# GpSimd instead of VectorE makes the low halves of the next group's weights in a hybrid GLA/SSD layer

## The chip, the cores and the metric

One core of a Trainium2 chip runs the kernel. The metric is the device time of one execution in microseconds: 1674.93 us as the median of three runs before the change (1674.78 to 1676.38).

## The reference

One decoder layer over 2048 tokens of width 1024, in float32. A conditioning vector gives shift, scale and gate; the normalised input h goes through one projection `w_in`, whose columns belong to two kinds of heads: gated linear attention (GLA) and a Mamba-2 state-space part (SSD). Their outputs go through `w_out`, a norm, the gate and a residual sum. The change concerns the SSD part and how its weights, and those of the last projection, are made ready:

```python
xbc = jax.nn.silu(causal_depthwise_conv(xbc, conv_w[i], conv_b[i]))
xs, Bm, Cm = jnp.split(xbc, [SSD_INNER, SSD_INNER + SSD_GROUPS * SSD_STATE], axis=-1)
dt = jax.nn.softplus(dt_raw.astype(f32) + dt_bias[i].astype(f32))
...
y = ssd_chunked(xs_h, dt, A, Bm..., Cm...)       # per chunk of 128: decay-weighted C B^T x, plus C times state
y = y + d_skip[i].astype(f32)[:, None] * xs_h
y = y.reshape(Bsz, T, SSD_INNER).astype(x.dtype) * jax.nn.silu(z)
y = rms_norm(y.reshape(Bsz, T, SSD_GROUPS, SSD_INNER // SSD_GROUPS), ...)
mixed = jnp.concatenate([o, y], axis=-1) @ w_out[i]
```

## The kernel before, in words

**Three stages.** `front` does the norms, the GLA projections and the GLA heads, `ssd` (the recurrence) the SSD heads, `project_out` the product with `w_out` and the end. In the trace the recurrence lies from about 755 to 1372 us.

**Split matrices.** Each matrix product is made of three float32r products of halves: a number is split into a high part (a copy rounded by ScalarE) and a low part (the number minus its high part), and high*high, high*low and low*high are summed. `w_high` (L1580, ScalarE) makes the high part of a unit of weights, `w_low` (L1707, VectorE) the low part. `h_high` and `h_low` do the same for quarters of the activations h.

**Blocks and units.** The recurrence goes over two groups of SSD heads (g = 0, 1), and in each over 8 blocks of 256 tokens, so 16 blocks n = 0 to 15, and a tail step 16. In block n TensorE makes 8 units for the current tokens: units 0 to 5 (B, C and four of x; 128 columns of weights each, 24 matmuls of 256 columns), and two z units (u = 6, 7; 24 matmuls of 512 columns). Between these units it does the recurrence of block n - 1, for its two tiles of 128 tokens, t = 0 and 1: `tile_in(0)` ahead of unit 0, `tile_out(0)` and `tile_in(1)` ahead of unit 2, `tile_out(1)` ahead of unit 4, `turn(0)` (the transposes of the normalised row block c_yn, L1930) ahead of unit 6, `turn(1)` at the end. Each engine's program is written out in this order by the same loop over u, and each executes its own in order; semaphores tie them.

**ScalarE in a block** (L1654): after unit u it evacuates the bank (`evacuate`: copies to c_before and c_acc, L1607 and L1609); TensorE's unit u + 2 waits for that, since there are two banks. Then, only in the last block of a group, `w_high` of the next group's unit u (in block 15, where the next stage's weights are made, `w_high(G, u - 1)`). Then, in some slots, `h_high`, `square` (u = 3 and 5) and `normed` (u = 4 and 6), which makes c_yn out of the c_rstd of GpSimd.

**VectorE in a block** (L1807): `tile_in` (c_xdt, c_xd, c_decay, c_btok), three taps of convolution for each unit (`convolve`, L1741), `tile_out` (c_yi, c_state, c_yt, twice), `segments` (16 instructions, L1802), `h_low`, and, in the last block of a group, `w_low` right behind the convolution of each unit.

**GpSimd in a block's recurrence** (L1556): for each tile `ends` (c_xend), `decay_state` (c_decayed, once c_state is ready), `skip` (c_yi + c_xd, once VectorE has made c_yi); then `rstd_of` for both tiles (c_mse, c_rstd, once ScalarE's square is there), then c_y_diff. GpSimd's step r belongs to the recurrence of block r, which the other engines do beside the units of block r + 1.

**Loads.** SyncE issues all loads in one order (L1477). w_raw has two slots; `load_w(g, u)` goes to slot u % 2 and waits until the low part of unit u - 2 has been made (`wait(sp, w_ready, order(g, u) - 1)`, L1436). In block 7 it issues loads 0, 1, 2, then a quarter of h, load 3, a quarter, loads 4 and 5, a quarter, load 6, a quarter, load 7. Units of w_in are 128x1024 (512 KB), those of the projection's w_sums 128x512 (256 KB). Units 6 and 7 of group 1 are z parts; their low parts are made in block 8.

Of the kernel before, what the change touches and what calls it, by code (L numbers as in the profile page):

```python
# [17 lines left out]
F32 = mybir.dt.float32  # L18
# [3 lines left out]
ALU = mybir.AluOpType  # L22
# [3 lines left out]
HI, LO = 0, 1  # L26
# [5 lines left out]
def wait(eng, sem, count):  # L32

    if not isinstance(count, int) or count > 0:
        eng.wait_ge(sem, count)
# [1306 lines left out]
def ssd(nc, sems, handed, y_stored, unit_done, h_ready, xd_ready, w_rows, w_sum_d, conv_col, convb_col, d_row, norm_col, ps, ident, tok, w, w_raw, hl_all, halves, w_even,  # L1342
        h_d, ac_d, y_d, column, T, KT, G, HG, GW, XT, NS, SP_, INNER, VAL, TAPS, B2, TB2):

    UB, UC, UX, UZ = 0, 1, 2, 2 + XT
# [3 lines left out]
    S = T // B2  # L1349
# [7 lines left out]
    NF = KT  # L1357
    with ExitStack() as ctx:
# [3 lines left out]
        def sem(name):  # L1362
            return sems.enter_context(nc.semaphore(name))
# [35 lines left out]
        w_hi = sem("c_w_hi"); w_ready = sem("c_w_ready"); unit_out = sem("c_unit_out")  # L1399
# [14 lines left out]
        def part(u, p):  # L1414

            return w[:, u, :, p, :] if u < UZ else w_z[:, :, p, (u - UZ) * P:(u - UZ + 1) * P]
# [5 lines left out]
        def order(g, u):  # L1422

            return u - UZ if g == 0 else g * U - UZ + u
# [87 lines left out]
        def gpsimd(pool):  # L1512
            pool.wait_ge(handed["att_done"], handed["last_scores"])
            pool.wait_ge(handed["again_low"], handed["h_parts"])
            pool.memset(past[:, :], 0.0).then_inc(consts_ready, 1)
            pool.memset(before[:, :, 0:HIST], 0.0).then_inc(consts_ready, 1)
            pool.wait_ge(consts_ready, 2)
            pool.affine_select(out=past[:, :], in_=past[:, :], compare_op=ALU.is_ge, fill=-1e30,
                               base=0, pattern=[[1, P]], channel_multiplier=-1).then_inc(consts_ready, 1)
            pool.wait_ge(handed["y_stored"], handed["all_y"])  # L1520
            pool.memset(neg_half[:, :], -0.5).then_inc(consts_ready, 1)
            pool.wait_ge(consts_ready, 4)

            def ends(r, g, b, t):

                m = r * TB2 + t
                pool.wait_ge(xdt_ready, m + 1)
                wait(pool, st_done, m)
                end = tok[:, bass.ds(b * TB2 + t, 1), 3, g * HG:(g + 1) * HG].rearrange("p a h -> p (a h)")
                pool.tensor_tensor(xend[:, :, :], xdt[:, :, :], end.unsqueeze(2).broadcast_to([P, HG, SP_]),  # L1530
                                   ALU.mult).then_inc(xend_ready, 1)

            def decay_state(r, g, t):
                m = r * TB2 + t
                pool.wait_ge(decay_ready, r + 1)
                pool.wait_ge(state_ready, m + g + 1)
                pool.tensor_tensor(decayed[:, :, :], state[:, :, :], chunk[:, :, t:t + 1].broadcast_to([P, HG, SP_]),
                                   ALU.mult).then_inc(decayed_ready, 1)

            def skip(r, t):  # L1540

                m = r * TB2 + t
                pool.wait_ge(xd_ready, m + 1)
                pool.wait_ge(yi_ready, m + 1)
                pool.tensor_tensor(yi[:, :, :], yi[:, :, :], xd[:, :, :], ALU.add).then_inc(skip_ready, 1)  # L1545

            def rstd_of(r, t):
                m = r * TB2 + t
                pool.wait_ge(ms_ready, m + 1)
                pool.sem_inc(passed, 1)  # L1550
                pool.tensor_scalar(mse[:, t:t + 1], ms[:, t:t + 1], EPS, None, ALU.add).then_inc(mse_ready, 1)
                pool.wait_ge(mse_ready, m + 1)
                wait(pool, yn_ready, m)
                pool.tensor_tensor(rstd[:, t:t + 1], mse[:, t:t + 1], neg_half[:, :], ALU.pow).then_inc(rstd_ready, 1)  # L1554

            def step(r, g, b):  # L1556

                for t in range(TB2):
                    ends(r, g, b, t)
                    decay_state(r, g, t)  # L1560
                    skip(r, t)
                for t in range(TB2):
                    rstd_of(r, t)
                pool.wait_ge(y_ready, r * TB2 + TB2)
                wait(pool, y_stored, r * 32)
                pool.tensor_tensor(y_diff[:, :, :], y[:, 0], y[:, 1], ALU.subtract).then_inc(diff_ready, 1)

            for g in range(G):
                step(g * S, g, 0)
                with pool.Fori(1, S) as i:  # L1570
                    step(i + g * S, g, i)

        def scalar(act):

# [131 lines left out]
        def vector(dve):  # L1706
            def w_low(g, u):  # L1707
                dve.wait_ge(w_hi, order(g, u) + 1)
                if g < G:
                    dve.tensor_tensor(part(u, LO), w_raw[:, u % 2], part(u, HI).bitcast(F32),  # L1710
                                      ALU.subtract).then_inc(w_ready, 1)
                else:
                    dve.tensor_tensor(w_even[:, u, LO, :], w_raw[:, u % 2, 0:KT // 2].rearrange("p k n -> p (k n)"),
                                      w_even[:, u, HI, :].bitcast(F32), ALU.subtract).then_inc(w_ready, 1)
# [41 lines left out]
            def tile_in(r, g, b, t):  # L1756
                m = r * TB2 + t
                dve.wait_ge(x_done, m + 1)
                wait(dve, y_done, m)
                wait(dve, xend_ready, m)  # L1760
                dve.tensor_tensor(xdt[:, :, :], bank(X), per_head(b, t, 0, g), ALU.mult).then_inc(xdt_ready, 1)  # L1761
                wait(dve, skip_ready, m)
                skips = d_row[:, g * HG:(g + 1) * HG].unsqueeze(2).broadcast_to([P, HG, SP_])
                dve.tensor_tensor(xd[:, :, :], bank(X), skips, ALU.mult).then_inc(xd_ready, 1)
                dve.wait_ge(bc_done, m + 1)
                dve.wait_ge(decay_ready, r + 1)
                dve.tensor_tensor(decay[:, :, t * P:(t + 1) * P], ps[:, BC, NS:NS + P].unsqueeze(1).broadcast_to([P, HG, P]),  # L1767
                                  decay[:, :, t * P:(t + 1) * P], ALU.mult)
                wait(dve, st_done, m)
                dve.tensor_copy(btok[:, :], ps[:, BC, 0:NS]).then_inc(wt_ready, 1)  # L1770

            def clear_state(r):
                wait(dve, yi_done, r * TB2)
                wait(dve, decayed_ready, r * TB2)
                dve.memset(state[:, :, :], 0.0).then_inc(state_ready, 1)
# [31 lines left out]
            def step(n, g, b, par, rg, rb, first_of_group, last_of_group):  # L1807


                going, back = g is not None, rg is not None  # L1810
                if back and first_of_group:
                    clear_state(n - 1)
                if isinstance(n, int) and n == 1:
                    dve.wait_ge(handed["y_stored"], handed["all_y"])
                for u in range(UP):
                    if back and u == 0:
                        tile_in(n - 1, rg, rb, 0)
                    if back and u == 2:
                        tile_out(n - 1, rg, rb, 0, 1 - par)
                        tile_in(n - 1, rg, rb, 1)  # L1820
                    if back and u == 4:
                        tile_out(n - 1, rg, rb, 1, 1 - par)
                    if g == 0 and rg is None and u in Z_SLOTS[0]:
                        w_low(0, UZ + Z_SLOTS[0].index(u))
                    if going and u < UZ:
                        convolve(n, g, u)
                        if u == UZ - 1:
                            history(n, last_of_group)
                    if going and u == UZ:
                        segments(n, g, b)  # L1830
                    if g == 1 and rg == 0 and u in Z_SLOTS[1]:
                        w_low(1, UZ + Z_SLOTS[1].index(u))
                    if last_of_group and g + 1 < G and u < UZ:
                        w_low(g + 1, u)
                    if last_of_group and g + 1 == G and u > 0:
                        w_low(G, u - 1)
                    if not going and u == 0:
                        w_low(G, NF - 1)
                    if back and u in H_SLOTS:
                        h_low(n + 1, H_SLOTS.index(u), 1 - par)  # L1840
# [13 lines left out]
        def tensor(pe, part):  # L1854
# [107 lines left out]
            step(G * S, None, 0, G - 1, 0)  # L1962

        return sync, gpsimd, scalar, vector, tensor


# [319 lines left out]
```

## Time and profile before

| | |
|---|---|
| median of three runs (lowest to highest) | 1674.93 us (1674.78 to 1676.38) |
| span of the profiled execution | 1675.5 us; the page gives no other time for it |
| TensorE busy | 1612.1 us, 96% of the span |
| VectorE busy | 1052.7 us, 63% |
| ScalarE busy | 841.1 us, 50% |
| GpSimd busy | 396.7 us, 24% |
| DMA, mean | 138 GB/s |

The shares are averages over three stages. A profile of this kind is to be read stage by stage: the stretches of single blocks, then what TensorE waited for in them, then each engine's instructions in order of time. In the rows a start in us stands first, then the time that the merged instructions took, the engine, the line, the operation, output and inputs, the count, and in brackets the idle time just before and what ended it.

### The profile page before, as it was taken

How to read it: one execution, taken by the hardware profiler on the slowest of the kernel's cores; microseconds unless marked ns; L12 is line 12 of the kernel's file. 1: busy time of each engine (PE TensorE's matmuls, PEld its weight loads, DVE VectorE, ACT ScalarE, POOL GpSimd, SP SyncE). 2: the span in 40 equal slices, each digit the busy share in tenths (PEclk: the TensorE clock that was granted, in tenths of full speed). 3: DMA queues.
4: the chain of work that ended last, by engine and by line, in shares of the span. 5: the costliest groups of instructions: out<-in, count | busy, mean ns of one | idle time of the engine just before them, and what ended most of it. 6: DMA issues, size and time to landing. Idle time of an engine off the chain costs nothing. (4 is left out here: it accounts for less than half of the span.)

```text
span 1675.5 us, 27425 instructions
## 1 busy us (share of the span) xinstructions
PE 1612.1 (96%) x9990; PEld 1387.5 (83%) x9990; DVE 1052.7 (63%) x1754; ACT 841.1 (50%) x1496; POOL 396.7 (24%) x449
## 2 busy tenths in 40 slices
PE   5999999999999999998999998999999999999997
PEld 4888888888888888888888887888888878888886
DVE  5545354465444554456777777867777754785996
ACT  5755555545544554464454555555454554234332
POOL 2311000101322222200223222223233220450423
PEclk9899999999999999999999999999999999999999
DMA  9423442264434533334222225322212326765886
GB/s 327 134 93 108 143 125 65 79 189 145 157 126 135 189 121 129 124 104 145 76 71 76 75 75 152 112 85 99 76 69 75 108 97 210 241 237 169 291 288 199
DMA packets 131358, 231.14 MB, mean 138 GB/s; under 512 B 9907, under 2 KB 81859, under 8 KB 126134
## 3 DMA queue, kind: packets, MB, share of 16 engines
q1 hardware_dynamic: 123910, 190.76, 35.2%
q10 hardware_dynamic: 6512, 38.80, 6.2%
q0 software_dynamic: 832, 0.22, 0.3%
q8 instruction: 62, 1.02, 0.2%
q14 instruction: 42, 0.34, 0.1%
HBM read 177.05 MB, written 52.70 MB: 137 GB/s over the span
## 5 line engine op out<-in xcount | busy, mean ns | idle before, releaser
L1155 PE MATMUL ps<-hl,w 128*128 128x512 f32 x1488 | 374.5, 401 | 0.1
L1155 PEld LDWEIGHTS ps<-hl,w 128*128 128x128 f32 x1488 | 275.1, 189 | 56.8 <-issue 1.4
L1870 PE MATMUL ps<-hl,w 128*128 128x256 f32 x2304 | 293.0, 287 | 0.0
L1870 PEld LDWEIGHTS ps<-hl,w 128*128 128x128 f32 x2304 | 280.6, 192 | 7.9 <-issue 7.8
L1161 PE MATMUL ps<-w,hl 128*128 128x256 f32 x1536 | 200.6, 287 | 0.0
L1161 PEld LDWEIGHTS ps<-w,hl 128*128 128x128 f32 x1536 | 190.6, 191 | 2.3
L1874 PE MATMUL ps<-hl 128*128 128x512 f32 x768 | 180.9, 395 | 4.5 <-DVE hl L1710 4.5
L1741 DVE SCALAR_TENSOR_TENSOR c_acc<-c_before,conv_col,c_acc 128x256 f32<-128x256 f32 x288 | 161.5, 563 | 36.9 <-ACT c_acc L1609 30.0
L1874 PEld LDWEIGHTS ps<-hl 128*128 128x128 f32 x768 | 144.7, 190 | 34.5 <-DVE hl L1710 4.7
L2259 PE MATMUL ps<-w,hl 128*128 128x512 f32 x720 | 164.1, 389 | 0.0
L2259 PEld LDWEIGHTS ps<-w,hl 128*128 128x128 f32 x720 | 135.0, 188 | 28.2 <-issue 0.3
L485 POOL TENSOR_SCALAR mse<-ms 128x1 f32<-128x1 f32 x60 | 15.6, 260 | 543.2 <-ACT squares L655 543.2
L1607 ACT ACTIVATE c_before<-ps 128x256 f32<-128x256 f32 x96 | 36.9, 384 | 209.2 <-PE ps L1870 209.2
L2259 PE MATMUL ps<-hl 128*128 128x512 f32 x576 | 131.0, 389 | 0.0
L2259 PEld LDWEIGHTS ps<-hl 128*128 128x128 f32 x576 | 108.1, 188 | 22.5
L902 DVE SCALAR_TENSOR_TENSOR state<-state,dec,ps 128x256 f32<-128x256 f32 x56 | 26.9, 480 | 108.1 <-PE ps L1198 108.1
L841 DVE TENSOR_TENSOR hl<-x_sb,hl 128x1024 fp32r<-128x1024 f32 x48 | 59.3, 1235 | 56.5 <-ACT hl L639 56.5
L2215 DVE TENSOR_TENSOR d_mixed<-d_mixed,ps 128x512 f32<-128x512 f32 x64 | 42.5, 683 | 53.3 <-PE ps L2259 34.5
L1545 POOL TENSOR_TENSOR c_yi<-c_yi,c_xd 128x512 f32<-128x512 f32 x32 | 41.4, 1293 | 131.7 <-DVE c_yi L1781 131.7
L914 DVE SCALAR_TENSOR_TENSOR y<-ps,norm_col,gz 128x128 f32<-128x128 f32 x120 | 36.3, 344 | 56.1 <-PE ps L1206 35.7
L852 DVE TENSOR_TENSOR w<-w_raw,w 128x1024 fp32r<-128x1024 f32 x30 | 37.5, 1252 | 50.2 <-ACT w L585 50.1
L1802 DVE SCALAR_TENSOR_TENSOR c_decay<-c_ac,tok,c_past 128x128 f32<-128x128 f32 x256 | 68.6, 347 | 0.1
(247 smaller groups left out, 2613.8 us busy)
## 6 DMA issues: line engine op xcount, KB each, us to landing
x_sb<-h SPq DMA_DIRECT2D x52, 512.0 KB, 3.9
w_raw<-in_w_in SPq DMA_DIRECT2D x44, 512.0 KB, 4.7
c_ac<-step_sums ACTq DMA_DIRECT2D x16, 1024.0 KB, 4.6
d_a_raw<-mixed_in SPq DMA_DIRECT2D x29, 512.0 KB, 4.1
c_h_raw<-h SPq DMA_DIRECT2D x56, 256.0 KB, 2.9
d_a_raw<-mixed_in SPq DMA_DIRECT2D x11, 1024.0 KB, 5.0
w_sums<-late ACTq DMA_DIRECT2D x8, 1280.0 KB
w_raw<-w_sums SPq DMA_DIRECT2D x40, 256.0 KB, 3.4
```

Source lines behind the costliest of these rows:

```text
L841: last = dve.tensor_tensor(hl[:, n % 2, ks, LO, :], raw, hl[:, n % 2, ks, HI, :].bitcast(F32), ALU.subtract)
L852: dve.tensor_tensor(lo, w_raw[:, u % 2], hi.bitcast(F32), ALU.subtract).then_inc(w_ready, 1)
L1155: mm = pe.matmul(ps[:, PROJ + u % 2, :], w[:, u, k, a, :], hl[:, par, k, b, :], start=(k == 0 and i == 0), stop=(k == KT - 1 and i == 2))
L1161: mm = pe.matmul(ps[:, PROJ + u % 2, half * DV:(half + 1) * DV], hl[:, par, k, a, t * P:(t + 1) * P], w_v[:, k, b, :], start=(k == 0 and i ...
L1545: pool.tensor_tensor(yi[:, :, :], yi[:, :, :], xd[:, :, :], ALU.add).then_inc(skip_ready, 1)
L1607: act.activation(before[:, u, HIST:], ps[:, PROJ + u % 2, 0:B2], ACT.Copy)
L1741: op = dve.scalar_tensor_tensor(out=acc[:, u, :], in0=before[:, u, k:k + B2], scalar=conv_col[:, k, ch:ch + 1], in1=acc[:, u, :], op0=ALU. ...
L1802: last = dve.scalar_tensor_tensor(out=decay[:, h, t * P:(t + 1) * P], in0=ac[:, h, t * P:(t + 1) * P], scalar=own, in1=past[:, :], op0=ALU ...
L1870: mm = pe.matmul(ps[:, PROJ + u % 2, 0:B2], w[:, u, k, a, :], hl[:, par, k, b, :], start=(k == 0 and i == 0), stop=(k == KT - 1 and i == 2))
L1874: mm = pe.matmul(ps[:, PROJ + u % 2, :], hl[:, par, k, a, t * P:(t + 1) * P], w_z[:, k, b, :], start=(k == 0 and i == 0), stop=(k == KT - ...
L2215: last = dve.tensor_tensor(mixed[:, p, r, c, :], old, bank, ALU.add if how > 0 else ALU.subtract)
L2259: mm = pe.matmul(ps[:, j % 8, :], halves[:, j % 4, k, a, :], weight(i)[:, k, b, :], start=(k == 0 and q == 0), stop=(k == KT - 1 and q == 2))
```

## The change

In the steps of the recurrence that run beside the last block of a group (block 7, where group 0 gives way to group 1, and block 15, where group 1 gives way to the projection), GpSimd makes the low parts that VectorE made: units 0 to 5 of group 1's weights, and units 0 to 6 of the projection's. VectorE keeps the z parts of group 1 (made in block 8) and unit 7 of the projection (made in the tail), and waits ahead of the first of either until the counter w_ready has all the earlier ones. GpSimd's loop over blocks becomes shorter by two steps for each group, and these two are written out.

```diff
+            def w_low(g, u):
+                pool.wait_ge(w_hi, order(g, u) + 1)
...
+                pool.tensor_tensor(lo, raw, hi.bitcast(F32), ALU.subtract).then_inc(w_ready, 1)
+
-            def step(r, g, b):
+            def step(r, g, b, before_last):
 
                 for t in range(TB2):
                     ends(r, g, b, t)
                     decay_state(r, g, t)
+                    if before_last and t == 1:
+                        w_low(g + 1, 0)
                     skip(r, t)
                 for t in range(TB2):
+                    for u in ((1,), (2, 3))[t] if before_last else ():
+                        w_low(g + 1, u)
                     rstd_of(r, t)
+                for u in range(4, 6 if g + 1 < G else 7) if before_last else ():
+                    w_low(g + 1, u)
                 pool.wait_ge(y_ready, r * TB2 + TB2)
...
             for g in range(G):
-                step(g * S, g, 0)
-                with pool.Fori(1, S) as i:
-                    step(i + g * S, g, i)
+                step(g * S, g, 0, False)
+                with pool.Fori(1, S - 2) as i:
+                    step(i + g * S, g, i, False)
+                step(g * S + S - 2, g, S - 2, True)
+                step(g * S + S - 1, g, S - 1, False)
...
             def w_low(g, u):
                 dve.wait_ge(w_hi, order(g, u) + 1)
+                if g > 0 and u in (UZ, NF - 1):
+                    dve.wait_ge(w_ready, order(g, u))
...
-                    if last_of_group and g + 1 < G and u < UZ:
-                        w_low(g + 1, u)
-                    if last_of_group and g + 1 == G and u > 0:
-                        w_low(G, u - 1)
                     if not going and u == 0:
                         w_low(G, NF - 1)
```

The order of GpSimd's instructions in its step beside block 7, with the changed kernel's own line numbers (L1563 is the new low part; c_xend, c_decayed, c_yi are `ends`, `decay_state`, `skip`, here of tile 1):

```order
L1530 TENSOR_TENSOR c_xend<-c_xdt,tok 128x512
L1537 TENSOR_TENSOR c_decayed<-c_state,c_chunk 128x512
L1563 TENSOR_TENSOR w<-w_raw,w 128x8x128
L1545 TENSOR_TENSOR c_yi<-c_yi,c_xd 128x512
L1563 TENSOR_TENSOR w<-w_raw,w 128x8x128
L1551 TENSOR_SCALAR c_mse<-c_ms 128x1
L1554 TENSOR_TENSOR c_rstd<-c_mse,c_neg_half 128x1
L1563 TENSOR_TENSOR w<-w_raw,w 128x8x128 x2
```

Four of the six low parts are here: unit 0 ahead of the second tile's `skip`, unit 1 behind it, units 2 and 3 behind the first tile's c_rstd; 4 and 5 follow behind the second tile's.

VectorE's order in block 7, kernel before, from the first convolution (c_acc) to the first tile's c_yi:

```order
L1741 SCALAR_TENSOR_TENSOR c_acc<-c_before,conv_col,c_acc 128x256 x3
L1710 TENSOR_TENSOR w<-w_raw,w 128x8x128
L1741 SCALAR_TENSOR_TENSOR c_acc<-c_before,conv_col,c_acc 128x256 x3
L1710 TENSOR_TENSOR w<-w_raw,w 128x8x128
L1725 TENSOR_TENSOR hl<-c_h_raw,hl 128x2x256
L1781 TENSOR_TENSOR c_yi<-ps,tok 128x512
```

and the same place in the changed kernel, from the end of `tile_in(0)` to the first tile's c_yt:

```order
L1789 COPY c_btok<-ps 128x128
L1760 SCALAR_TENSOR_TENSOR c_acc<-c_before,conv_col,c_acc 128x256 x6
L1744 TENSOR_TENSOR hl<-c_h_raw,hl 128x2x256
L1800 TENSOR_TENSOR c_yi<-ps,tok 128x512
L1803 TENSOR_TENSOR c_state<-ps,c_decayed 128x512
L1807 TENSOR_TENSOR c_yt<-ps,c_yi 128x512
```

The two low parts that stood between the convolutions of units 0 and 1 and the first tile's c_yi are gone from VectorE. TensorE, ScalarE and SyncE keep their order.

## Rows read from the trace of the kernel before

**Rows 1.** Stretches (us, busy by engine, clock, DMA): loop step, block 7.

```profile
976.00:1012.24 36.24, 36.24 (x286) 31.63 (x285) 27.15 (x55) 18.74 (x37) 10.36 (x12) 1.00 0.23 79
...
1012.24:1052.45 40.21, 35.45 (x260) 29.81 (x260) 31.28 (x57) 21.84 (x38) 9.71 (x11) 0.96 0.52 151
```

**Rows 2.** TensorE in order of time, block 7: start, us, work, idle before it.

```profile
1029.74 1.88 PE L1917 MATMUL ps<-c_xdt,c_decay 128*64 128x64 f32 x32 [3.73 <-DVE c_btok L1770]
...
1040.16 0.66 PE L1930 MATMUL ps<-ident,c_yn 128*128 128x128 f32 x4 [0.88 <-ACT c_yn L1640]
...
1040.57 11.17 PE L1874 MATMUL ps<-hl 128*128 128x512 f32 x48
```

**Rows 3.** ScalarE in order of time, block 7.

```profile
1019.37 0.56 ACT L1609 ACTIVATE c_acc<-ps,convb_col,conv_col 128x256 f32<-128x256 f32 x1
...
1024.15 1.06 ACT L1585 ACTIVATE w<-w_raw 128x1024 fp32r<-128x1024 f32 x1 [1.41 <-DMA w_raw<-in_w_in]
...
1025.90 0.56 ACT L1609 ACTIVATE c_acc<-ps,convb_col,conv_col 128x256 f32<-128x256 f32 x1
...
1037.91 1.06 ACT L1585 ACTIVATE w<-w_raw 128x1024 fp32r<-128x1024 f32 x1 [0.63 <-DMA w_raw<-in_w_in]
...
1042.19 0.62 ACT L1633 ACTIVATE c_squares<-c_yt 128x512 bf16<-128x512 f32 x1
```

**Rows 4.** VectorE in order of time, block 7.

```profile
1013.26 3.03 DVE L1741 SCALAR_TENSOR_TENSOR c_acc<-c_before,conv_col,c_acc 128x256 f32<-128x256 f32 x3 [1.47 <-ACT c_acc L1609]
...
1019.23 1.23 DVE L1710 TENSOR_TENSOR w<-w_raw,w 128x1024 fp32r<-128x1024 f32 x1 [2.94 <-ACT w L1585]
...
1021.80 1.22 DVE L1710 TENSOR_TENSOR w<-w_raw,w 128x1024 fp32r<-128x1024 f32 x1
...
1027.08 0.69 DVE L1761 TENSOR_TENSOR c_xdt<-ps,tok 128x512 f32<-128x512 f32 x1
...
1032.98 1.52 DVE L1741 SCALAR_TENSOR_TENSOR c_acc<-c_before,conv_col,c_acc 128x256 f32<-128x256 f32 x3
...
1035.55 0.69 DVE L1781 TENSOR_TENSOR c_yi<-ps,tok 128x512 f32<-128x512 f32 x1
```

**Rows 5.** GpSimd in order of time, block 7.

```profile
1014.26 1.23 POOL L1537 TENSOR_TENSOR c_decayed<-c_state,c_chunk 128x512 f32<-128x512 f32 x1
...
1028.95 1.05 POOL L1537 TENSOR_TENSOR c_decayed<-c_state,c_chunk 128x512 f32<-128x512 f32 x1
...
1043.44 0.79 POOL L1554 TENSOR_TENSOR c_rstd<-c_mse,c_neg_half 128x1 f32<-128x1 f32 x1
```

**Rows 6.** GpSimd by line: ns min/median/max, first and last start.

```profile
L1566 POOL TENSOR_TENSOR c_y_diff<-c_y x16: 1284/1294/1302, 829.0 to 1373.4; 128x512 f32<-128x512 f32 x16
...
L2118 POOL TENSOR_TENSOR d_a_raw<-d_a_raw x16: 2391/2738/3133, 1428.2 to 1597.5; 128x1024 f32<-128x1024 f32 x16
```

**Rows 7.** Loads of w_raw, L1438 (512 KB), then L1440 (256 KB): issue to landing.

```profile
DMA to landing us min/median/max: 3.6/4.4/8.1
...
DMA to landing us min/median/max: 2.6/2.7/3.2
```

**Rows 8.** Order of time, block 15: VectorE, GpSimd, ScalarE, TensorE.

```profile
1332.51 0.69 DVE L1781 TENSOR_TENSOR c_yi<-ps,tok 128x512 f32<-128x512 f32 x1
...
1333.34 1.30 POOL L1545 TENSOR_TENSOR c_yi<-c_yi,c_xd 128x512 f32<-128x512 f32 x1 [5.31 <-DVE c_yi L1781]
...
1334.07 0.63 ACT L1588 ACTIVATE w<-w_raw 128x512 fp32r<-128x512 f32 x1
...
1336.41 0.66 PE L1930 MATMUL ps<-ident,c_yn 128*128 128x128 f32 x4 [0.23 <-ACT c_yn L1640]
```

**Rows 9.** TensorE's first z units, then a stretch behind the 3.73 us wait.

```profile
775.72 13.54 PE L1874 MATMUL ps<-hl 128*128 128x512 f32 x48 [4.52 <-DVE hl L1710]
...
1031.60:1033.00 1.40, 1.40 (x5) 0.79 (x3) 1.40 (x3) 0.00 (x0) 0.00 (x0) 0.50 0.00 0
```

**Rows 10.** TensorE in order of time, the tail behind block 15.

```profile
1362.73 1.15 PE L1917 MATMUL ps<-c_xdt,c_decay 128*64 128x64 f32 x32 [1.72 <-DVE c_btok L1770]
```

More of the change, by code:

```diff
@@ L1554, in rstd_of @@
                 pool.tensor_tensor(rstd[:, t:t + 1], mse[:, t:t + 1], neg_half[:, :], ALU.pow).then_inc(rstd_ready, 1)
-            def step(r, g, b):
+            def w_low(g, u):
+                pool.wait_ge(w_hi, order(g, u) + 1)
+                if g < G:
+                    hi, lo, raw = w[:, u, :, HI, :], w[:, u, :, LO, :], w_raw[:, u % 2]
+                else:
+                    hi, lo = w_even[:, u, HI, :], w_even[:, u, LO, :]
+                    raw = w_raw[:, u % 2, 0:KT // 2].rearrange("p k n -> p (k n)")
+                pool.tensor_tensor(lo, raw, hi.bitcast(F32), ALU.subtract).then_inc(w_ready, 1)
+            def step(r, g, b, before_last):
                 for t in range(TB2):
```

## The prediction, made before the changed kernel ran

> **What bounds the kernel now.** I read the stretches first, then the waits of TensorE, then the four compute engines in order of time around the two places where the change acts. Most steps of the recurrence are bound by TensorE: it is busy 36.24 of 36.24 us in a step of the loop [rows 1], and VectorE, ScalarE and GpSimd wait for it. The step in which group 0 gives way to group 1 (block 7; its `w_low` calls make the low halves of group 1's units 0 to 5) is different: TensorE is busy 35.45 of 40.21 us [rows 1]. Two gaps are named: 3.73 us before the y products, until VectorE has written c_btok, and 0.88 us before the transposes of c_yn [rows 2]. In the step before the projection (block 15) only 0.23 us are lost at the same transposes [rows 8]. So there is little to win, at most the two gaps.
>
> What the reader must see next is a ring that goes through those same engines. w_raw has two slots. The load of unit u+2 waits for the low part of unit u; ScalarE's `w_high(u+2)` waits for that load; and ScalarE works strictly in the order of its program, in which `w_high` stands between things TensorE needs: the evacuation of the next unit, `square`, `normed`. Before, low(0) ends at 1020.46 on VectorE and w_high(2) starts at 1024.15, having waited 1.41 us for the transfer; w_high(4) waited 0.63 us for its own [rows 3, 4]. The ring has no slack here already. Whatever delays low(0), (1), (2) by more than that delays ScalarE, and ScalarE's c_yn is what the TensorE queue stands behind at 1040.16 [rows 2].
>
> **What is removed.** VectorE loses 6 lows of 1.2 us in block 7 and 7 lows of 0.69 us in block 15. In block 7 only the first two lie ahead of c_btok: c_acc of unit 1 is done at 1019.37 + 0.56 = 1019.93 [rows 3], so convolve(1) starts some 0.4 us sooner, and low(1) gives 1.2. The 3.73 us wait becomes 2.1. That saving stays only if nothing later in the step is late; it isn't so.
>
> **What is added, block 7.** I follow the new order. On GpSimd low(0) stands behind xend(1) and decayed(1) of tile 1, not at unit 0. A GpSimd low of 128x1024 is not in the trace. A GpSimd subtraction or sum of the same size took 2.39 us at least and 2.74 as median; twice the 128x512 one is 2 x 1.294 = 2.6 [rows 6]. Bounds 2.4 and 3.1 (longest of the rows of that size); I take 2.6. From low's end to the start of `w_high` of the next unit in the slot I take 3.7 us (1020.46 to 1024.15 [rows 3, 4]); landing alone took 3.6 to 8.1, median 4.4 [rows 7], so 3.7 is near the low end, right for a load that has no other one beside it.
> 1. c_xdt(1) was at 1027.08 [rows 4], now 1.6 us earlier, 1025.5. decayed(1) ended at 1028.95 + 1.05 = 1030.0 [rows 5], now 1028.4. low(0) ends at 1031.0; I add 0.3 for its turns with VectorE: 1031.3, against 1020.46.
> 2. Load 2, 3.7 us: w_high(2) starts at 1035.0 (was 1024.15). h_high and c_acc(3) follow, 1025.90 + 0.56 - 1024.15 = 2.3 us after it [rows 3]: 1037.3. VectorE waits for it with h_low and convolve(3), 1.5 us [rows 4]: yi(1) at 1038.8 (was 1035.55).
> 3. `skip(1)` on GpSimd starts 0.83 us after yi and takes 1.3 (1332.51, 1333.34 [rows 8] show the pair): 1040.9. Only then low(1): 1043.5 (was 1023.0).
> 4. Load 3, 3.7 us: w_high(3) at 1047.2, one us of work, square(0) at 1048.2. `rstd_of` ends 2.0 us after the start of its square (1042.19 to 1043.44 + 0.79 [rows 3, 5]): 1050.2. low(2), queued behind it: 1052.8.
> 5. Load 4, 3.7 us: w_high(4) at 1056.5 (was 1037.91). From there to TensorE's c_yn transposes 2.25 us (1037.91 to 1040.16 [rows 2, 3]): 1058.8 against 1040.16, **18.6 us later**.
> Meanwhile TensorE does the y products, unit 4, waits for c_acc(3), does unit 5 until about 1040.3 and stands still for 18 us. Its order is fixed: the two z units behind the transposes can't go first. What comes after shifts with it: low(4) and (5) end near 1069, ahead of block 8, and loads 6 and 7 near 1067 and 1069, about 5 us later than the shift alone would make them; ScalarE needs their data at about 1056.59 + 18.6 + the clock's share, so they still land. VectorE's 16 segments lie beside lows 4 and 5; c_decay has some 2 us of room. Nothing more is charged.
>
> **The clock.** Behind today's 3.73 us wait a stretch shows a granted clock of 0.50, that is 1.2 instead of 2.4 GHz, and behind a 4.52 us wait at the first block the two z units took 13.54 us instead of 11.17 [rows 2, 9]. After 18 us idle the same fall before the same z units is due: 13.54 - 11.17 = 2.4 us more. The slow stretch inside today's step lies ahead of the new end of the chain, so its going or staying changes nothing. Block 7 in all: 18.6 + 2.4 = 21.0.
>
> **Block 15.** `w_high` stands one unit later, loads and lows are half the size. VectorE reaches yi(1) 1.5 us sooner (lows 0 to 2 are off it; 1332.51 to 1331.0), skip ends at 1333.1, low(1) of 1.3 us at 1334.4. A load of this size lands in 2.6 to 3.2 us [rows 7]; with its issue 3.0: w_high(3) at 1337.4 (was 1334.07). From there to the transposes it is the 2.25 us of block 7 less 0.43 for the half-sized w_high (1.06 and 0.63 [rows 3, 8]), 1.8: 1339.3 against 1336.41 [rows 8], +2.9. low(2) follows rstd(0) and its load lands near 1339.9, just when ScalarE is there. The 3.2 us gap may drop the clock: 0 to 2.4, I take 1.2. In the tail low(6) no longer stands ahead of c_xdt on VectorE, and of TensorE's 1.72 us wait there [rows 10] I give back 1.2. Block 15 in all: +2.9.
>
> **Sum.** 21.0 + 2.9 = 23.9. The profiled execution spans 1675.5 us, 0.6 above the median of 1674.93, so 1675.5 + 23.9 = 1699.4 in its terms, 1698.8 in those of the median: **1699**. Bounds: with lows of 2.4, no 0.3, no clock, block 15 at +1.0: 18.6 - 0.9 + 1.0 = 18.7. With three lows of 3.1 and three loads at 4.4: 18.6 + 1.5 + 2.1 + 2.4, and block 15 at +5.5: 30. This is 1693 to 1705.
>
> **The skill weighed against the row.** convolve(0), begun at 1013.26, took 3.03 us for three taps while GpSimd made c_decayed, against 1.52 alone [rows 4, 5]: VectorE is held up while GpSimd runs. The Trainium skill, SBUF — State Buffer, section "Who interferes with whom", says that a VectorE instruction with two SBUF inputs and a GpSimd one that reads SBUF exclude each other for a whole instruction, and the one that came first wins. The trace agrees in kind. By that rule each GpSimd low would also block VectorE for its 2.6 us, so moving 1.2 us of VectorE work costs VectorE more than it frees wherever it has work; here it mostly waits then. The sum by it alone would be at most 1 us higher for each of the lows 0 and 1, 1701.
>
> **Rivals.**
> - *The ring bites deeper* (14%). Lows at 3 us and over, loads over 4.4 us since they now meet the state and c_h_raw transfers, and block 15 loses its clock too: 28 to 34 us, 1703 to 1709; about 1706. For: landings up to 8.1 us [rows 7]. Against: there is one load in flight at a time now.
> - *It bites half* (11%). Only one round of the ring is felt, because low(1) goes before skip(1)'s input is late, or w_high(3) overlaps TensorE's wait: 8 to 14 us, about 1686. For: TensorE itself could be at the transposes at 1040 only. Against: each of the three rounds has its own GpSimd predecessor (decayed(1), skip(1), rstd(0)), and each of these waits for ScalarE or VectorE.
> - *Faster, the relief decides* (3%). VectorE's 3.73 us gap shrinks by 1.6, the slow clock behind it goes (1.6 us), the tail gives 1.2: 4.4 us, 1670.5. It decides if low(2) is done by 1034.2, that is w_high(4) no later than 1037.91. Against: low(0) alone can't start before 1028.
> - *Nothing is felt* (2%): the chain is hidden under z units, 1675. Against: the transposes stand ahead of the z units.
> - The forecast (70%): 1691 to 1706.
>
> **Chances.** 0.2% of the time is 3.3 us, about what can be told from no change. Faster 3%, same 2%, slower 95%. The range 1688 to 1707 leaves out the faster and the unchanged case, most of the half case and the tail of the deep one.
>
> **What would show it.** TensorE's wait for ACT c_yn near 18 us at the first place and 3 at the second; ScalarE's waits for `w_raw` of about 12 us before w_high(2), 10 before w_high(3), 6 before w_high(4); GpSimd rows of 2.6 and 1.3 us; 13.5 us for the z units of block 7. It is wrong if w_high(3) there starts less than 6 us after c_acc(3), or if low(0) starts before c_decayed(1).

## The result: 26 us slower

| | before | changed |
|---|---|---|
| median of four (lowest to highest) | 1674.86 us (1673.97 to 1676.38) | 1700.9 us (1700.78 to 1701.83) |
| span of the profiled execution | 1675.5 us | 1699.3 us |
| ratio of the runs | | 1.0152 (95% interval 1.014 to 1.0164) |

The forecast was 1699 with 1688 to 1707. The first rows of the page of the changed kernel: span, busy time of each engine, granted clock in 40 slices.

```profile
span 1699.3 us, 27402 instructions
...
PE 1615.4 (95%) x9990; PEld 1390.4 (82%) x9990; DVE 1053.7 (62%) x1741; ACT 841.1 (49%) x1496; POOL 421.8 (25%) x462
...
PEclk9999999999999999999999997999999999999999
```

TensorE's busy time is nearly what it was, GpSimd has 25 us more and VectorE as much as before, though 13 low halves (some 12 us) have left it: what it does beside GpSimd takes longer. The clock row has one slice at 7.

**Where the time is, by blocks.** Since the two profiled executions differ by 1.4 us before the change acts, I compare lengths. A block begins with TensorE's first transposes of c_xbc; for block 15 and the tail I take the last c_yn transposes of the block before.

| | before | changed | difference |
|---|---|---|---|
| block 7 | 43.48 (1008.54 to 1052.02) | 64.42 (1007.12 to 1071.54) | +20.9 |
| block 8 | 39.78 | 39.53 | -0.3 |
| blocks 9 to 14 | 219.44 | 219.44 | 0 |
| block 15 | 37.01 | 42.42 | +5.4 |
| tail, to the first product of the projection | 24.01 | 23.10 | -0.9 |

The sum is +25.2, between the difference of the spans (23.8) and that of the medians (26.0). Less the 1.4 us ahead of block 7 it is the difference of the spans. A span and a median of times can't be subtracted from each other, as the prediction did with its "0.6 above the median": in the later runs of the kernel before, an execution's time is 1.7 to 1.8 us more than its span, so by that estimate the profiled one took about 1677.2 us, over 2 us more than the median. The forecast itself starts from the median. The table also corrects a row of mine: the second stretch of [rows 1], called block 7, starts 3.7 us inside it and ends 0.4 us behind it. The block really took 43.5 us, 6.9 more than a step of the loop, so there was a little more to win than the prediction said. No term of its sum came from that row.

TensorE in block 7 of the changed kernel, in the columns of [rows 2]:

```profile
1026.78 1.15 PE L1932 MATMUL ps<-c_xdt,c_decay 128*64 128x64 f32 x32 [2.59 <-DVE c_btok L1789]
...
1028.42 3.43 PE L1885 MATMUL ps<-hl,w 128*128 128x256 f32 x24
...
1035.99 5.49 PE L1885 MATMUL ps<-hl,w 128*128 128x256 f32 x24 [4.14 <-ACT c_acc L1626]
...
1057.21 1.11 PE L1945 MATMUL ps<-ident,c_yn 128*128 128x128 f32 x4 [15.73 <-ACT c_yn L1657]
...
1057.97 13.29 PE L1889 MATMUL ps<-hl 128*128 128x512 f32 x48
...
1071.10 0.60 PE L1945 MATMUL ps<-ident,c_yn 128*128 128x128 f32 x4
```

The 3.73 us wait for c_btok of [rows 2] is now 2.59, then comes a wait that wasn't there, 4.14 us ahead of unit 5 for ScalarE's c_acc(3), and the wait ahead of the c_yn transposes is 15.73 us instead of 0.88. Unit 5 itself ran slowly (5.49 us against 3.1). The z units took 13.29 us instead of 11.17.

ScalarE, GpSimd and VectorE in the same block:

```profile
1033.63 1.06 ACT L1602 ACTIVATE w<-w_raw 128x1024 fp32r<-128x1024 f32 x1 [12.31 <-DMA w_raw<-in_w_in]
...
1035.38 0.56 ACT L1626 ACTIVATE c_acc<-ps,convb_col,conv_col 128x256 f32<-128x256 f32 x1
...
1046.01 1.06 ACT L1602 ACTIVATE w<-w_raw 128x1024 fp32r<-128x1024 f32 x1 [10.08 <-DMA w_raw<-in_w_in]
...
1046.97 0.61 ACT L1650 ACTIVATE c_squares<-c_yt 128x512 bf16<-128x512 f32 x1
...
1054.97 1.06 ACT L1602 ACTIVATE w<-w_raw 128x1024 fp32r<-128x1024 f32 x1 [6.57 <-DMA w_raw<-in_w_in]
...
1056.45 0.71 ACT L1657 ACTIVATE c_yn<-c_yt,c_rstd 128x512 f32<-128x512 f32 x1
```

```profile
1025.88 1.05 POOL L1537 TENSOR_TENSOR c_decayed<-c_state,c_chunk 128x512 f32<-128x512 f32 x1
...
1026.88 2.55 POOL L1563 TENSOR_TENSOR w<-w_raw,w 128x1024 fp32r<-128x1024 f32 x1
...
1038.24 1.28 POOL L1545 TENSOR_TENSOR c_yi<-c_yi,c_xd 128x512 f32<-128x512 f32 x1 [8.81 <-DVE c_yi L1800]
...
1039.47 2.37 POOL L1563 TENSOR_TENSOR w<-w_raw,w 128x1024 fp32r<-128x1024 f32 x1
...
1048.18 0.57 POOL L1554 TENSOR_TENSOR c_rstd<-c_mse,c_neg_half 128x1 f32<-128x1 f32 x1
...
1048.71 4.88 POOL L1563 TENSOR_TENSOR w<-w_raw,w 128x1024 fp32r<-128x1024 f32 x2
```

```profile
1011.84 3.03 DVE L1760 SCALAR_TENSOR_TENSOR c_acc<-c_before,conv_col,c_acc 128x256 f32<-128x256 f32 x3 [1.47 <-ACT c_acc L1626]
...
1024.11 0.68 DVE L1780 TENSOR_TENSOR c_xdt<-ps,tok 128x512 f32<-128x512 f32 x1
...
1026.64 3.59 DVE L1760 SCALAR_TENSOR_TENSOR c_acc<-c_before,conv_col,c_acc 128x256 f32<-128x256 f32 x3
...
1037.41 0.68 DVE L1800 TENSOR_TENSOR c_yi<-ps,tok 128x512 f32<-128x512 f32 x1
...
1060.09 8.60 DVE L1821 SCALAR_TENSOR_TENSOR c_decay<-c_ac,tok,c_past 128x128 f32<-128x128 f32 x16
```

This is the ring, step by step. L1563 is GpSimd's low half; "low(0)" is short for the low half of unit 0, c_yi(1) for c_yi of tile 1. low(0) begins at 1026.88 behind c_decayed(1); w_high(2) (L1602) has then waited 12.31 us for its transfer, and VectorE's c_yi(1) comes at 1037.41. `skip(1)` lets low(1) begin at 1039.47; w_high(3) has waited 10.08. Its square gives c_rstd at 1048.18, low(2) begins at 1048.71; w_high(4) has waited 6.57. c_yn follows at 1056.45, and TensorE goes on at 1057.21. In [rows 3] the waits before w_high(2) and (4) were 1.41 and 0.63 us.

The clock of the first part of the z units (columns as in [rows 1]; the clock is the figure third from the end):

```profile
1057.30:1061.00 3.70, 3.70 (x11) 3.12 (x12) 2.95 (x9) 3.70 (x7) 0.77 (x2) 0.50 0.25 71
```

It is 0.50, the lower of the two levels (1.2 instead of 2.4 GHz), behind the long wait.

Block 15 of the changed kernel, in the engines' order of [rows 8], then the tail:

```profile
1346.47 2.50 DVE L1760 SCALAR_TENSOR_TENSOR c_acc<-c_before,conv_col,c_acc 128x256 f32<-128x256 f32 x3
...
1350.93 0.68 DVE L1800 TENSOR_TENSOR c_yi<-ps,tok 128x512 f32<-128x512 f32 x1
...
1351.76 1.29 POOL L1545 TENSOR_TENSOR c_yi<-c_yi,c_xd 128x512 f32<-128x512 f32 x1 [3.58 <-DVE c_yi L1800]
...
1353.01 1.30 POOL L1563 TENSOR_TENSOR w<-w_raw,w 128x512 fp32r<-128x512 f32 x1
...
1357.65 0.63 ACT L1605 ACTIVATE w<-w_raw 128x512 fp32r<-128x512 f32 x1 [4.19 <-DMA w_raw<-w_sums]
...
1359.46 1.11 PE L1945 MATMUL ps<-ident,c_yn 128*128 128x128 f32 x4 [4.01 <-ACT c_yn L1657]
...
1360.23 12.42 PE L1889 MATMUL ps<-hl 128*128 128x512 f32 x48
...
1386.63 1.15 PE L1932 MATMUL ps<-c_xdt,c_decay 128*64 128x64 f32 x32 [0.90 <-DVE c_btok L1789]
```

The transposes waited 4.01 us, the z units behind them took 12.42 us (11.15 in the profile before), and the tail's wait for c_btok fell from the 1.72 us of [rows 10] to 0.90.

### The profile page after: what moved, and what is told of

Same layout as the page of the kernel before. It is cut to its first block and busy times, and to the rows that moved or that the text cites. A ratio compares the mean times of both kernels' runs of the same rounds, so it can differ in the third digit from the quotient of the medians.

```text
span 1699.3 us, 27402 instructions
## 1 busy us (share of the span) xinstructions
PE 1615.4 (95%) x9990; PEld 1390.4 (82%) x9990; DVE 1053.7 (62%) x1741; ACT 841.1 (49%) x1496; POOL 421.8 (25%) x462
## 3 DMA queue, kind: packets, MB, share of 16 engines
q1 hardware_dynamic: 123910, 190.76, 34.9%
## 5 line engine op out<-in xcount | busy, mean ns | idle before, releaser
L1760 DVE SCALAR_TENSOR_TENSOR c_acc<-c_before,conv_col,c_acc 128x256 f32<-128x256 f32 x288 | 168.6, 587 | 47.4 <-ACT c_acc L1626 40.4
L1821 DVE SCALAR_TENSOR_TENSOR c_decay<-c_ac,tok,c_past 128x128 f32<-128x128 f32 x256 | 74.0, 365 | 0.1
L1780 DVE TENSOR_TENSOR c_xdt<-ps,tok 128x512 f32<-128x512 f32 x32 | 22.0, 687 | 77.6 <-PE ps L1913 77.6
```

The costliest lines, as they stand in the source:

```text
L1760: op = dve.scalar_tensor_tensor(out=acc[:, u, :], in0=before[:, u, k:k + B2], scalar=conv_col[:, k, ch:ch + 1], in1=acc[:, u, :], op0=ALU. ...
L1821: last = dve.scalar_tensor_tensor(out=decay[:, h, t * P:(t + 1) * P], in0=ac[:, h, t * P:(t + 1) * P], scalar=own, in1=past[:, :], op0=ALU ...
```

## The experiments

The theory to be tested (A): the place of the low halves in GpSimd's program makes the ring of load, high half and low half late, and ScalarE, which stands in it in front of the evacuations and of c_yn, hands that to TensorE. The rivals: (B) a low half on GpSimd lasts twice as long and holds VectorE up, and that costs wherever it stands; (C) the weights themselves come late.

### One place at a time

Only block 7 (against the changed kernel), and the mirror of it for block 15:

```diff
-                step(g * S + S - 2, g, S - 2, True)
+                step(g * S + S - 2, g, S - 2, g == 0)
...
+                    if last_of_group and g + 1 == G and u > 0:
+                        w_low(G, u - 1)
```

> Only block 7's low halves are on GpSimd, block 15's are back on VectorE. By the traces block 7 costs 20.9 us and block 15 4.5: 1674.9 + 20.9 = 1695.8 (1694.5 to 1697.5). If the two places interact (what block 7 delays is caught up or paid again later) it lies outside.

Measured: 1695.49 us (1693.86 to 1695.68), the kernel before beside it 1674.49; ratio 1.0125 (1.0108 to 1.0142). +21.0, as expected.

> Only block 15's low halves are on GpSimd, block 7's are back on VectorE: 1674.9 + 4.5 = 1679.4 (1678 to 1681). If block 15's effect is only the clock behind a wait that block 7 prepared, it is under 1 us.

Measured: 1679.64 us (1678.2 to 1681.28), ratio 1.0028 (1.0017 to 1.0039). +5.2, and its block 15 is 41.59 us long, 4.6 over before, with a tail 0.9 shorter, so that its trace places 3.7 of the 5.2. In the changed kernel block 15 was 0.8 longer still: from the end of low(1) to w_high(3) it took 3.3 us there and 2.6 here (1335.14 to 1337.76). The two runs add up to 26.2, the cost of both changes together, so within the spread of the runs the places don't interact.

### The same late places, but no low half on GpSimd

Against the kernel before:

```diff
                         tile_out(n - 1, rg, rb, 1, 1 - par)
+                        if last_of_group and g + 1 < G:
+                            w_low(g + 1, 1)
...
-                    if last_of_group and g + 1 < G and u < UZ:
-                        w_low(g + 1, u)
+                    if last_of_group and g + 1 < G:
+                        if u == 2:
+                            dve.wait_ge(decayed_ready, (n - 1) * TB2 + 2)
+                            w_low(g + 1, 0)
+                        if u == 4:
+                            dve.wait_ge(rstd_ready, (n - 1) * TB2 + 1)
+                            w_low(g + 1, 2)
+                            w_low(g + 1, 3)
+                        if u == 5:
+                            dve.wait_ge(rstd_ready, (n - 1) * TB2 + 2)
+                            w_low(g + 1, 4)
+                            w_low(g + 1, 5)
```

> VectorE makes block 7's low halves, but at the points at which GpSimd made them in the changed kernel: low(0) once c_decayed(1) is there, (1) behind tile_out(1), (2) and (3) once the first c_rstd is there, (4) and (5) once the second is; block 15 as before the change. Theory A: the ring is as late though no low half is on GpSimd: low(0) and (1) end at the same time as there, (2) 1.3 us sooner: +17 and 2 for the clock, 1674.9 + 19 = 1694 (1690 to 1697). Theory B: GpSimd's duration and the holding up of VectorE are gone, so at most 1680.

Measured: 1696.41 us (1694.43 to 1697.24), ratio 1.0132 (1.0115 to 1.0149): +21.9, as much as with GpSimd in block 7. VectorE's low halves (L1710), ScalarE's w_high(2), (3), (4) (L1585) and TensorE's transposes:

```profile
1025.90 1.22 DVE L1710 TENSOR_TENSOR w<-w_raw,w 128x1024 fp32r<-128x1024 f32 x1
...
1038.58 1.22 DVE L1710 TENSOR_TENSOR w<-w_raw,w 128x1024 fp32r<-128x1024 f32 x1
...
1047.79 2.35 DVE L1710 TENSOR_TENSOR w<-w_raw,w 128x1024 fp32r<-128x1024 f32 x2
...
1031.27 1.06 ACT L1585 ACTIVATE w<-w_raw 128x1024 fp32r<-128x1024 f32 x1 [12.22 <-DMA w_raw<-in_w_in]
...
1043.92 1.06 ACT L1585 ACTIVATE w<-w_raw 128x1024 fp32r<-128x1024 f32 x1 [10.35 <-DMA w_raw<-in_w_in]
...
1052.92 1.06 ACT L1585 ACTIVATE w<-w_raw 128x1024 fp32r<-128x1024 f32 x1 [6.60 <-DMA w_raw<-in_w_in]
...
1055.16 1.12 PE L1942 MATMUL ps<-ident,c_yn 128*128 128x128 f32 x4 [18.39 <-ACT c_yn L1640]
```

The three waits are 12.22, 10.35 and 6.60 us, those of the changed kernel within 0.3. Its block 7 (from 1004.85) is 64.47 us long, against 64.42. Counted from the beginning of the block, the low halves compare like this:

| | start of low(0), (1), (2) | end of low(0), (1), (2) |
|---|---|---|
| GpSimd, changed kernel | 19.8, 32.4, 41.6 | 22.3, 34.7, 44.0 |
| VectorE, this run | 21.1, 33.7, 42.9 | 22.3, 34.9, 44.1 |

VectorE needs half the time, but in this order it gets to each low half 1.3 to 1.4 us later, and the ends are the same within 0.2. (The expectation had low(2) end 1.3 us sooner, but it stands behind a convolution; that is a part of why 21.9 was measured and not 19.) So a late end costs the same whichever engine makes the low half, and with no low half on GpSimd there is nothing to hold VectorE up: that part of B isn't needed for block 7. GpSimd's longer operation isn't ruled out as a part of the lateness. In the changed kernel the three low halves took 7.4 us on GpSimd, and on VectorE from the same starts they would have taken 3.7; by this estimate up to 3.7 of the 18.5 us of delay are duration and the rest is place. No run separates the two. The shorter loops of GpSimd's program aren't a cause either: this run doesn't have them and is as slow, and the last run below has them without this cost.

### GpSimd, but as early as the high halves allow

Against the changed kernel:

```diff
+            LOWS = (((0, 1), (2,), (3,), (), (4,), (5,)), ((0,), (1,), (2,), (), (3,), (4, 5, 6)))
...
-                    if before_last and t == 1:
-                        w_low(g + 1, 0)
+                    lows(t)
+                    if t == 1:
+                        lows(2)
                     skip(r, t)
                 for t in range(TB2):
-                    for u in ((1,), (2, 3))[t] if before_last else ():
-                        w_low(g + 1, u)
+                    lows(3 + t)
                     rstd_of(r, t)
...
+                lows(5)
```

> GpSimd makes the same low halves as in the changed kernel, but each as soon as ScalarE has made the high half: in block 7 low(0) and low(1) ahead of skip(0), low(2) ahead of skip(1), low(3) right behind it, (4) behind the first c_rstd, (5) last; in block 15 low(0) ahead of skip(0), (1) and (2) ahead of skip(1), (3) behind the first c_rstd. Theory A (the place in GpSimd's order closes the ring through the two w_raw slots): nearly all of the 26 us goes; VectorE is held up by low(0) and (1), so 2 to 6 us over the kernel before, 1677 to 1681, and ScalarE's wait before w_high(2) falls from 12.3 to about 2 us. Theory B (a low half of 2.5 us instead of 1.2, and VectorE held up while GpSimd runs, are what costs, wherever they stand): 1693 or more.

Measured: 1682.44 us (1681.47 to 1684.41), ratio 1.005 (1.0033 to 1.0067). 18 of the 26 us are gone; +8 stays, more than the 2 to 6 I expected. TensorE in block 7:

```profile
1024.74 1.13 PE L1930 MATMUL ps<-c_state,c_xbc 128*128 128x512 f32 x2 [2.05 <-DVE c_state L1808]
...
1029.58 1.98 PE L1937 MATMUL ps<-c_xdt,c_decay 128*64 128x64 f32 x32 [3.72 <-DVE c_btok L1794]
...
1042.66 0.66 PE L1950 MATMUL ps<-ident,c_yn 128*128 128x128 f32 x4 [2.97 <-ACT c_yn L1662]
...
1043.08 11.15 PE L1894 MATMUL ps<-hl 128*128 128x512 f32 x48
```

VectorE's convolutions of units 1 and 2:

```profile
1017.81 5.07 DVE L1765 SCALAR_TENSOR_TENSOR c_acc<-c_before,conv_col,c_acc 128x256 f32<-128x256 f32 x3 [3.58 <-ACT c_acc L1631]
...
1029.45 5.56 DVE L1765 SCALAR_TENSOR_TENSOR c_acc<-c_before,conv_col,c_acc 128x256 f32<-128x256 f32 x3
```

The wait of 15.73 us is 2.97, and ScalarE's before w_high(2) fell to 2.67, but a 2.05 us wait for c_state is new, the 3.72 us for c_btok stands as before, and c_yn is late by 2.97 instead of 0.88. Block 7 is 48.02 us long (+4.5), block 15 37.98 (+1.0), the tail 24.62 (+0.6); these and block 8 make 6.5 of the 8, the rest isn't placed. The 4.5 of block 7 are VectorE held up, the second half of B. Three taps take 5.07 us beside low(0) and (1), and VectorE reaches `h_low` 1.9 us later in the block than before, which is what c_state and c_btok are late by. The next three take 5.56 us beside low(2) and (3), both of which are ahead of skip(1), and cost 2.7 us more: SyncE issues load 4 behind a quarter of h that waits for `h_low`, so w_high(4) and c_yn come late. So B is real too where TensorE waits for VectorE; in the changed kernel's block 7 VectorE was waiting itself.

### ScalarE's high halves later

Against the run with only block 7 on GpSimd:

```diff
-                        if last and g + 1 < G and u < UZ:
+                        if last and g + 1 < G and u < 2:
                             w_high(g + 1, u)
...
                         normed(n - 1, 0)
+                    if last and g + 1 < G and u == 4:
+                        w_high(g + 1, 2)
+                    if last and g + 1 < G and u == 5:
+                        w_high(g + 1, 3)
                     if back and u == 5:
                         square(n - 1, 1)
...
+                    if last and g + 1 < G and u == 6:
+                        w_high(g + 1, 4)
...
+                    if last and g + 1 < G and u == 7:
+                        w_high(g + 1, 5)
```

> As the run with only block 7's low halves on GpSimd, in the changed kernel's GpSimd order, but ScalarE makes block 7's high halves 2 to 5 later: (2) behind normed(0), (3) ahead of square(1), (4) behind the evacuation of unit 6, (5) behind that of unit 7. The ring load, high, low is as long as before; ScalarE no longer stands in it ahead of the evacuations and of c_yn. Theory A (the ring reaches TensorE through ScalarE's order): the 21 us go nearly all, 1674.5 + 1 to 2 = 1676 (1673 to 1679). Theory C (the weights themselves come late, wherever ScalarE waits): the lateness shows at block 8's units, 1690 or more.

Measured: 1679.75 us (1677.38 to 1680.73), the kernel before beside it 1675.68; ratio 1.0023 (1.0013 to 1.0033). Of the 21 us 17 are gone, with GpSimd's program untouched. TensorE's transposes of block 7, its units and c_btok wait of block 8, then ScalarE's c_yn and w_high(2):

```profile
1038.68 0.66 PE L1955 MATMUL ps<-ident,c_yn 128*128 128x128 f32 x4 [2.50 <-ACT c_yn L1657]
...
1055.84 3.10 PE L1895 MATMUL ps<-hl,w 128*128 128x256 f32 x24 [1.50 <-ACT c_z L1631]
...
1073.29 1.15 PE L1942 MATMUL ps<-c_xdt,c_decay 128*64 128x64 f32 x32 [3.01 <-DVE c_btok L1797]
...
1037.91 0.72 ACT L1657 ACTIVATE c_yn<-c_yt,c_rstd 128x512 f32<-128x512 f32 x1 [3.20 <-POOL c_rstd L1554]
...
1038.54 1.04 ACT L1602 ACTIVATE w<-w_raw 128x1024 fp32r<-128x1024 f32 x1
```

c_yn now comes first and w_high(2) behind it, with no wait left for its transfer. Block 7 is 43.83 us long, 0.35 over before. But block 8 is 44.20, 4.4 over: TensorE waits 1.50 us for ScalarE's c_z and 3.01 for c_btok there, since high half (4) pushes ScalarE's c_decay and with it c_z back, and high half (5), low(5) and c_y_diff lie in it. What is put off is paid for later, in part. This isn't C: TensorE waits there for c_z, c_xend, c_btok and c_yn, and the trace puts none of its waits down to a weight. In all it is 4.1 over the kernel before instead of 1 to 2: the mechanism was right, what it is paid with in block 8 was left out.

### Loads sooner, and both together

Against the kernel before, all low halves on VectorE:

```diff
                 if group_ends:
-                    for u in (0, 1, 2):
-                        load_w(g + 1, u)
+                    load_w(g + 1, 2)
...
+                if isinstance(s, int) and s == S - 2:
+                    for u in (0, 1):
+                        load_w(g + 1, u)
                 if not (isinstance(s, int) and s == 0):
                     store_y(n - 1, g, s - 1)
```

> The kernel before (all low halves on VectorE), with loads 0 and 1 of the next weights issued one step earlier, behind the last quarter of h of the step before, so that w_high(0) in block 7 doesn't wait 4.9 us for its transfer. Theory: convolve(1) and with it c_btok come 2.6 us sooner, and the slow clock behind the 3.7 us wait goes (1.6 us): 1674.5 - 4 = 1670.5 (1669 to 1672). If low(0) and (1) on VectorE alone make the wait, it stays near 1674.

Measured: 1671.67 us (median of 11 runs; the kernel before beside it 1675.68), ratio 0.9982 (0.9973 to 0.9991): **faster than the kernel before**, by 3 us by the ratio and 4 by the medians. w_high(0), w_high(4) and TensorE's two waits in block 7:

```profile
1010.42 1.06 ACT L1587 ACTIVATE w<-w_raw 128x1024 fp32r<-128x1024 f32 x1
...
1032.26 1.06 ACT L1587 ACTIVATE w<-w_raw 128x1024 fp32r<-128x1024 f32 x1 [2.27 <-DMA w_raw<-in_w_in]
...
1024.04 1.15 PE L1919 MATMUL ps<-c_xdt,c_decay 128*64 128x64 f32 x32 [1.13 <-DVE c_btok L1772]
...
1034.50 0.66 PE L1932 MATMUL ps<-ident,c_yn 128*128 128x128 f32 x4 [2.51 <-ACT c_yn L1642]
```

w_high(0) has no wait. c_btok is waited for 1.13 us instead of 3.73, and the slow clock behind it is gone. c_yn is waited for 2.51 us instead of 0.88, so that block 7 is 40.51 us long: 3.0 less than before, not 4. What the step gained at one wait came partly back at the next, since w_high(4) waits 2.27 us for its transfer: SyncE issues load 4 behind a quarter of h that waits for VectorE's `h_low`.

Together with later high halves and GpSimd's low halves (low(1) and (2) behind the first c_rstd, (3) to (5) behind the second):

```diff
-                    for u in ((1,), (2, 3))[t] if before_last else ():
-                        w_low(g + 1, u)
+                    if t == 1 and before_last:
+                        w_low(g + 1, 1)
+                        w_low(g + 1, 2)
                     rstd_of(r, t)
-                for u in range(4, 6 if g + 1 < G else 7) if before_last else ():
+                for u in (3, 4, 5) if before_last else ():
```

> Early loads and the later high halves together, block 7's low halves on GpSimd: (0) behind c_decayed(1), (1) and (2) behind the first c_rstd, (3) to (5) behind the second; high half (3) behind silu_conv; block 15's low halves on VectorE. VectorE has no low half ahead of c_btok(1): of the 6.9 us by which block 7 is longer than a step of the loop (43.5 against 36.6) some 5 go: 1669.5 (1667.5 to 1672). If GpSimd's low halves hold VectorE up ahead of c_yi(1) as much as they free it, it is no faster than the run with early loads alone.

Measured: 1675.04 us (1673.33 to 1676.76), ratio 0.9997 (0.9988 to 1.0006), no change from before and 3.4 us slower than early loads alone. TensorE in block 8:

```profile
1050.96 4.51 PE L1898 MATMUL ps<-hl,w 128*128 128x256 f32 x24 [2.39 <-ACT c_z L1634]
...
1068.57 1.49 PE L1945 MATMUL ps<-c_xdt,c_decay 128*64 128x64 f32 x32 [2.63 <-DVE c_btok L1800]
```

The expectation missed. Its rival named the outcome, no faster than early loads alone, but not the cause: block 7 is 37.80 us long, 5.7 less than before, as near to a step of the loop as hoped, but block 8 is 45.23, 5.5 more. The work that GpSimd and ScalarE put off lands in the block in which the z parts are to be split; TensorE waits there for c_z and c_btok, as in the run with the later high halves.

## Why the prediction was right

- **The chain of block 7** was predicted as 18.6 us of delay at the c_yn transposes. Counted from the first convolution (1013.26 before, 1011.84 changed), it is (1057.21 - 1011.84) - (1040.16 - 1013.26) = 18.5. The terms erred in opposite ways: GpSimd's three low halves took 2.55, 2.37 and 2.4 us, not 2.6 and 0.3 for turns; from the end of one to the next `w_high` it was 4.2, 4.2 and about 3.9 us (1029.43 to 1033.63, 1041.84 to 1046.01, 1051.1 to 1054.97), not 3.7. That they cancel to 0.1 us is luck; the order of the steps isn't. The prediction's 3.7 was "right for a load that has no other one beside it", but a quarter of h is issued right behind loads 2 and 3.
- **ScalarE's waits** were given as about 12, 10 and 6 us: 12.31, 10.08, 6.57. TensorE's for c_yn was to be near 18 and shows as 15.73: the slow clock fell on unit 5, which took 2.4 us longer and ended that much later. In the run with only block 7 changed it fell on unit 4 instead, and the wait was 17.96. For the time this is the same.
- **The clock** was given 2.4 us in block 7: from the transposes of tile 0 to those of tile 1 it was 13.89 us instead of 11.42, so 2.5. In block 15 I had taken 1.2 as the middle of 0 and 2.4: it was 13.03 instead of 11.40, so 1.6.
- **Block 15** was the term that was mis-sized: +2.9 predicted, +4.5 measured. The delay at the transposes is 3.8 us instead of 2.9: VectorE reached c_yi(1) 0.85 us sooner and not 1.5, because three taps took 2.50 us beside GpSimd's low(0) instead of 1.73 at that place before, and a load took 3.3 us and not 3.0. The clock gave 0.4 more than I took, and the tail returned 0.9 and not 1.2.
- **VectorE held up.** Three taps took 3.59 us beside low(0) and 5.44 beside low(2) and (3), and the 16 segments 8.60 us beside low(4) and (5), against 1.52 and 4.30 in the kernel before. What they took more is 0.8 to 0.9 of the time of the low halves beside them. This agrees with the rule of the Trainium skill, SBUF — State Buffer, section "Who interferes with whom", that a VectorE instruction with two SBUF inputs contends with a GpSimd instruction that reads SBUF. The prediction put up to 1 us more for each of two low halves by it. In block 7 nothing of this reached the end, since the blocked VectorE was about to wait anyway; in block 15 it is the 0.65 us by which c_yi(1) came later than predicted.
- **Rivals.** The half case fell: all three rounds of the ring were felt, each behind its own GpSimd predecessor. The faster case gained nearly what was computed for it at its place (c_btok came 1.5 us sooner after the first convolution; the wait for it fell only to 2.59 us and not 2.1, because TensorE was there sooner too; no slow clock followed), and lost it in the ring. The deeper case wanted low halves of 3 us and loads over 4.4; they took at most 2.55 and 4.2.
- The measured 1700.9 is 2 us over the forecast; 1.6 of it are block 15 with its clock and tail, the rest isn't placed.

## What to carry to other kernels

An instruction that frees a buffer must end, in its new engine's program, no later than it ended before: ask what is queued ahead of it there, and who issues the next load and who waits for it in order. Each instruction moved in block 7 was 1.2 us of work; the late ends of three of them cost 18.5 us before the clock, and as much when VectorE made them equally late. Made early on GpSimd instead, the low halves cost 4.5 us there, because they hold up VectorE where TensorE waits for it. Loads issued sooner gained 3 to 4 us with no work moved at all. An engine that is 24% busy isn't free if what it has in its queue waits for the others.

## What the runs showed of the hardware

- In the changed kernel GpSimd subtracts 128x1024 into float32r in 2.37 to 2.55 us and 128x512 in 1.26 to 1.46; VectorE took 1.22 and 0.69 before. The two-input rows of 128x1024 on GpSimd before the change had a median of 2.74 [rows 6].
- Work of VectorE and GpSimd that overlaps holds the other up both ways: the 16 segments took 8.60 us instead of 4.30 beside two low halves, and in the last run one low half of GpSimd that began amid the segments took 4.63 us.
- TensorE's granted clock fell to 0.50 behind waits of 3.73, 3.72 and 2.86 us (matmuls of 1.13 us took 1.98 to 2.08 behind them), of 2.51 (1.72) and 2.49 (1.63), and of 2.39 in block 8 of the last run (24 matmuls took 4.51 instead of 3.1). It stayed at 1.00 behind waits of 2.59 in the changed kernel, 2.50 and 2.51 ahead of the c_yn transposes of two runs, and 2.97 there in the early run (z units 11.15 us). The length of a wait alone didn't decide it in these rows.
- A gap of 15.7 us cost no more clock (2.5 us) than one of 4.5 (2.4, [rows 9]).
